# Attention softmax: shift writes negated scores and takes their minimum, and the weighting takes the sum's reciprocal and the gate itself

## The reference, cut to what matters

```
s = q . k - slope * distance
s = where(mask, s, NEG_INF)
m = max(s, axis=-1)
p = where(mask, exp(s - m), 0.0)
p = p / max(sum(p), 1e-30)
o = gate_c * o_c + gate_s * (p_s @ v_s) + gate_w * (p_w @ v_w)
```

## Time and profile before

| what | value |
|---|---|
| median of three runs | 1402.91 us (1398.88 to 1407.49) |
| the profiled execution | 1410.37 us |
| its span, first to last instruction | 1407.4 us |
| TensorE busy | 1309.8 us, 93% of the span |
| VectorE busy | 835.1 us, 59% |
| ScalarE busy | 408.9 us, 29% |
| GpSimd busy | 818.4 us, 58% |
| attention loop | about 889 to 1070 us of the span |
| line 1882, two instructions for each unit | 57.5 us busy, 128 instructions |
| line 1156 | 70.4 us busy, 128 instructions |
| mean granted clock of TensorE | 0.969 of 2.4 GHz |

### The profile page before, as it was taken

How to read it: one execution, slowest core, us unless ns; L and a number is a source line. 1 busy time by engine, 2 the same in 40 slices (tenths; PEclk the granted TensorE clock), 3 DMA queues, 4 the chain that set the end, 5 groups by cost and what they waited for, 6 DMA issues and landing times.

```text
span 1407.4 us, 22999 instructions
## 1 busy us (share of the span) xinstructions
PE 1309.8 (93%) x8136; PEld 1040.3 (74%) x8136; DVE 835.1 (59%) x1464; ACT 408.9 (29%) x782; POOL 818.4 (58%) x1041
## 2 busy tenths in 40 slices
PE   6999789899999999999989999898988998999986
PEld 4778688678887788888778797555556787878874
DVE  6977895569789311597418344577773649632223
ACT  4265100434301133212200121666673201231111
POOL 7677101587899877899776718100002875357862
PEclk9999898999999999999999999899999999999998
DMA  5222100143325433345492303000004459423321
GB/s 193 77 75 80 31 3 1 53 133 98 97 82 187 135 120 97 100 148 157 149 319 78 92 16 97 9 1 1 1 1 161 125 146 267 178 69 96 97 82 67
DMA packets 86480, 137.94 MB, mean 98 GB/s; under 512 B 16512, under 2 KB 34432, under 8 KB 85376
## 3 DMA queue, kind: packets, MB, share of 16 engines
q1 hardware_dynamic: 48384, 88.10, 20.7%
q10 hardware_dynamic: 38016, 48.71, 10.8%
HBM read 119.02 MB, written 20.91 MB: 99 GB/s over the span
## 4 chain that ended last, share of the span: by engine, by line
PE 74%; DVE 11%; issue 5%; POOL 3%; ACTq 3%; ACT 2%; DMA 2%; POOLq 0%; DVEq 0%
PE ps L373 18%; PE ps L374 18%; PE ps L375 18%; PE ps L718 3%; PE ps L730 3%; PE ps L707 2%; ACTq L1053 2%; POOL small L1286 1%; DVE acc L1360 1%; DVE bigB L1882 1%; PE ps L543 1%; PE ps L611 1%; PE ps L656 1%; PE ps L787 1%; PE ps L535 1%
## 5 line engine op out<-in xcount | busy, mean ns | idle before, releaser
L1289 POOL TENSOR_TENSOR wl<-raw,wh 128x512 fp32r<-128x512 f32 x336 | 497.6, 1481 | 26.9
L1286 POOL TENSOR_TENSOR small<-small 1x1 f32<-1x1 f32 x336 | 119.5, 356 | 340.4 <-PE ps L375 335.1
L373 PE MATMUL ps<-uH,wh 128*128 128x512 f32 x672 | 267.9, 399 | 17.6 <-DVE uL L1350 10.8
L375 PE MATMUL ps<-uH,wl 128*128 128x512 f32 x672 | 263.9, 393 | 0.0
L374 PE MATMUL ps<-uL,wh 128*128 128x512 f32 x672 | 263.9, 393 | 0.0
L1287 POOL CAST wh<-raw 128x512 fp32r<-128x512 f32 x336 | 203.3, 605 | 0.0
L373 PEld LDWEIGHTS ps<-uH,wh 128*128 128x128 f32 x672 | 127.6, 190 | 47.7 <-POOL wl L1289 9.9
L374 PEld LDWEIGHTS ps<-uL,wh 128*128 128x128 f32 x672 | 127.8, 190 | 27.4 <-issue 1.4
L375 PEld LDWEIGHTS ps<-uH,wl 128*128 128x128 f32 x672 | 127.6, 190 | 27.0
L373 PE MATMUL ps<-ffH,wh 128*128 128x512 f32 x256 | 101.3, 396 | 4.4 <-POOL wl L1289 4.3
L374 PE MATMUL ps<-ffL,wh 128*128 128x512 f32 x256 | 99.8, 390 | 0.0
(11 more groups left out here) (382 smaller groups left out, 2482.6 us busy)
## 6 DMA issues: line engine op xcount, KB each, us to landing
raw<-wstream SPq DMA_DIRECT2D x336, 256.0 KB, 2.6
b_powers_scratch<-bigB ACTq DMA_DIRECT2D x4, 1024.0 KB, 4.7
c_powers_scratch<-bigB ACTq DMA_DIRECT2D x8, 512.0 KB, 4.1
lags_scratch<-lag_rows_scratch ACTq DMA_DIRECT2D x8, 512.0 KB, 9.4
bigB<-b_powers_scratch ACTq DMA_DIRECT2D x4, 1024.0 KB, 8.2
bigB<-lags_scratch ACTq DMA_DIRECT2D x4, 1024.0 KB, 8.7
bigB<-c_powers_scratch ACTq DMA_DIRECT2D x4, 1024.0 KB, 11.3
hT<-x ACTq DMA_DIRECT2D x4, 512.0 KB, 7.4
```

The lines of the kernel that those rows point to most:

```text
L373: pe.matmul(out, lh, rh, start=first, stop=False)
L375: return pe.matmul(out, ll, rh, start=False, stop=last)
L1286: pool.tensor_tensor(small[0:1, 569 + j:570 + j], zero_ap[0:1], zero_ap[0:1], ALU.add)
L1289: pool.tensor_tensor(wl[:, j, :], raw[:, j, :], wh[:, j, :].bitcast(f32), ALU.subtract).then_inc(half_split, 1)
```

## The change

`shift` passes the factor -1.0 and the minimum where it passed 1.0 and the maximum, with the initial value +3e38. The instruction computes (scores + penalty) x factor and reduces that, so `prob` now holds the negated scores, and the reduced value is the negated maximum itself. It goes directly into `anmax`; line 1887, `amax` and the semaphore `at_m` are gone. ScalarE waits for `at_s` instead and computes exp(-1.0 x prob + anmax), which is the same number.

In `weigh` the multiplication of the reciprocal by the gate is gone. The scaling of the probabilities multiplies by two per-partition values, first the reciprocal, then the gate.

```diff
-                    act.wait_ge(at_m, n + 1)
+                    act.wait_ge(at_s, n + 1)
                     for half in range(2):
-                        i = act.activation(prob[:, n % 3, half, 0:W], prob[:, n % 3, half, 0:W], ACT.Exp,
+                        i = act.activation(prob[:, n % 3, half, 0:W], prob[:, n % 3, half, 0:W], ACT.Exp, scale=-1.0,
                                            bias=anmax[:, n % 3, half:half + 1], accum_out=asum[:, n % 3, half:half + 1])
...
                 for half in range(2):
                     i = dve.tensor_tensor_reduce(prob[:, u % 3, half, 0:W], ps[:, u % 2 * 2 + half, 0:W],
-                                                 dsl[t % 2][:, half, 512 - W:512], 1.0, -3e38, ALU.add, ALU.max,
-                                                 amax[:, u % 3, half:half + 1])
+                                                 dsl[t % 2][:, half, 512 - W:512], -1.0, 3e38, ALU.add, ALU.min,
+                                                 anmax[:, u % 3, half:half + 1])
                 i.then_inc(at_s, 1)
-                dve.wait_ge(at_s, u + 1)
-                dve.tensor_scalar(anmax[:, u % 3, :], amax[:, u % 3, :], -1.0, None, ALU.mult).then_inc(at_m, 1)
...
                 own(dve.reciprocal(asum[:, u % 3, :], asum[:, u % 3, :]))
-                own(dve.tensor_tensor(asum[:, u % 3, :], asum[:, u % 3, :], gate[:, qt, 1 + b, t::KT], ALU.mult))
                 for half in range(2):
-                    i = dve.tensor_scalar(prob[:, u % 3, half, 0:W], prob[:, u % 3, half, 0:W], asum[:, u % 3, half:half + 1], None, ALU.mult)
+                    i = dve.tensor_scalar(prob[:, u % 3, half, 0:W], prob[:, u % 3, half, 0:W], asum[:, u % 3, half:half + 1],
+                                          gate[:, qt, 1 + b, half * KT + t:half * KT + t + 1], ALU.mult, ALU.mult)
                 i.then_inc(at_p, 1)
```

More of the change, by code:

```diff
@@ L216, in build @@
         cm, cs_ = small[:, 500:516], small[:, 516:532]
-        amax = small[:, 532:538].rearrange("p (u b) -> p u b", b=2)
         anmax = small[:, 538:544].rearrange("p (u b) -> p u b", b=2)
@@ L268, in build @@
         ds_ready = sem("slopes_ready")
-        at_qk, at_s, at_m, at_e, at_p, at_t, at_ev, at_v, at_o = (sem(f"att_{n}") for n in
-            ("scores", "scores_read", "max", "exp", "probs", "transposed", "probsT", "value", "out"))
+        at_qk, at_s, at_e, at_p, at_t, at_ev, at_v, at_o = (sem(f"att_{n}") for n in
+            ("scores", "scores_read", "exp", "probs", "transposed", "probsT", "value", "out"))
         s_bc = sem("ssm_bc_loaded")
```

## The result

| | before | changed |
|---|---|---|
| median | 1402.75 us (1398.87 to 1407.49, 8 runs) | 1391.97 us (1388.92 to 1395.79, 8 runs) |
| profiled execution, its span | 1410.37, 1407.4 us | 1388.92, 1387.1 us |
| mean granted clock of it | 0.969 | 0.979 |

The ratio is 0.9923, 95% interval 0.9899 to 0.9946: 10.8 us less, where 8.6 were forecast. The difference is under 1%, but the interval leaves out 1. The time lies in the forecast's own bounds, 1390.7 to 1397.5.

What follows compares the result with a forecast made beforehand. TensorE, three quarters of the chain, bounded the kernel and waited 19.7 us for VectorE's scaled probabilities. Savings of 1.00 us for each t, 8.0 for eight, plus first and last unit made 8.6: 1402.9 to 1394 us, range 1386 to 1402.

Steps and rivals of the forecast that it cites:

- accumulator read to first scaling: In VectorE's weigh, the time between these two falls from 0.59 to 0.28 us, each unit's way 0.31 shorter.
- second pointer, both scalings of a unit: Each scaling in weigh reads a second per-partition value, costing 0 to 0.11 us a unit; 0.06 taken.
- turn(2): TensorE's wait for scaled probabilities at unit 2 (units 0 to 7) of each t: 0.51 us, coming 0.25 earlier.
- turn(4): TensorE's wait at unit 4: savings of weigh(2), (3) and (4) add up to 0.75 of 0.51 + 0.40 us.
- turn(6), GpSimd quiet: TensorE's wait at unit 6 without GpSimd interfering: 0.86 us before, coming another 0.25 earlier.
- turn(6) beside GpSimd: Six of the eight waits at unit 6, beside two GpSimd operations: 1.60 us each, saving 0.25 (0 to 0.6).
- first unit, last unit: At the two ends of the attention loop: the first unit saves about 0.33 us, the last 0.25.
- The ceiling: TensorE's 24 waits at line 718 for scaled probabilities, 19.7 us, the most a shorter VectorE can give directly.
- one of the signs: In VectorE's scaling: the prediction would be wrong if the 512-column scaling left 0.48 us.
- the clock rival: In the loop, shorter turn(6) waits remove two to four half-clock stretches, 5 to 10 us on top, 1388; chance 0.25.
- The slower rival: Two pointers push VectorE's scaling off its double rate: 4 to 6 us slower, 1408; chance 0.08.
- Nothing comes through: Behind each TensorE wait something else stands ready, ScalarE's copy or GpSimd, with added clock stretches: 1402 us; chance 0.12.

Runs made afterwards that it cites:

- e9: The changed kernel again, in 9 runs on one more chip: 1393.73 us against 1401.65 for the kernel before, ratio 0.9937, 7.9 us less.
- e10: The kernel before, unedited, executed once more for a second trace: 1397.19 us.
- experiments 1 and 2: The two halves of the change, each alone on the kernel before (e1 and e2): 1396.73 and 1398.03 us.
- e7: The kernel before with GpSimd's penalties two units later and four small dependent VectorE operations added in weigh(6): 1406.57 us, ratio 1.0024.
- e5: The changed kernel with a constant 0.5 in place of the gate's pointer in the scaling, leaving the gate out: 1388.44 us, ratio 0.9893.
- e1: The kernel before with the negated scores only, the gate still multiplied onto the reciprocal: 1396.73 us, ratio 0.9929.
- e2: The kernel before with only the gate multiply moved into the scaling, the negation kept: 1398.03 us, ratio 0.9942.
- e6: The changed kernel with GpSimd's penalties started two units later: 1387.85 us, ratio 0.9893 to the kernel before.

## Why the prediction was right, step by step

| step | forecast | measured |
|---|---|---|
| accumulator read to first scaling | 0.59 to 0.28 us | to 0.20 |
| second pointer, both scalings of a unit | 0.06 (0 to 0.11) | 0.12 |
| net for each unit | 0.25 | 0.27 |
| minimum for maximum | 0 | 0 (421 for 422 ns) |
| turn(2) | 0.25 | 0.27 |
| turn(4) | 0.50 (0.75 with turn(2)) | 0.40 (0.67); 0.26 in the first t |
| turn(6), GpSimd quiet | 0.25 | 0.27 |
| turn(6) beside GpSimd | 0.25 (0 to 0.6) | 0.23 |
| one t, no GpSimd | 1.00 | 0.94 |
| first unit, last unit | 0.33, 0.25 | 0.26, 0 |
| TensorE's waits in the loop | about 12 us | 12.9 (12.7 in e9) |
| VectorE busy | 21 less, minus the pointers' 7.7 | 13.6 less |
| sum | 8.6 | 7.4 in waits (20.3 in e10 to 12.9), 7.5 in full-clock time |

**The mechanism held.** At full clock the gain comes from the places named, each within 0.1 us of its share but for two: turn(4) of the first t, and the last unit, behind which TensorE does not wait for the scaling before or after the change. The row of before that was farthest from the operation, the 57 ns of a first pointer, was the price of the second one within 3 ns.

**Two errors hid each other.** The reciprocal was given 0.08 us behind the accumulator read and took 0.00, which made the unit's way 0.08 shorter than thought. For the pointer it took the middle between free and twice 57 ns, 0.06 a unit, and the upper end was the true one, 0.12. So the net was 0.39 less 0.12, where the forecast had 0.31 less 0.06: 0.27 for 0.25, right here partly by luck.

**The term that was mis-sized is turn(4).** Three savings of 0.25 were added up in front of it, 0.75, against 0.51 + 0.40 of waits. But turn(2) had taken its 0.27 already, and what turn(4) still waited was 0.40, not 0.50, and in the first t only 0.26. A saving beyond that only makes VectorE early. That is 0.9 of the 1.2 us by which the sum was high; the last unit, 0.25, is nearly all of the rest. In experiments 1 and 2 the cap shows as the 0.8 us at turn(4) by which the whole change saves less than its two halves added up.

**The ceiling and one of the signs.** The 19.7 us named as the ceiling were 20.3 without the swallowed wait. The 24 waits are three in each t, but in the first t they are not at turn(2), turn(4) and turn(6): there they are at turn(0), turn(4) and turn(6), and the swallowed one at turn(1), which gave the 0.27 that turn(2) did not. And one sign of being wrong came true without meaning it: the 512-column scaling left 0.48 and takes 0.54 with GpSimd quiet. The prediction's own price of 57 ns for a pointer would have put it there, so the sign contradicted the sum; it belonged at the 0.6 that the rival names.

**The surplus of the first comparison.** It gave 10.8 us and the second one 7.9. The shorter waits explain 7.4. In the second the clock's part is 1.3 us (33.2 for 34.5), not told from none. For the first the clocks of the kernel before are not on record except for the profiled execution, so that its 3 us more are clock is likely and not shown: the mean clock's share of the kernel before was 34.5, 36.1 and 39.7 us on three chips, and that of the changed kernel 32.5 and 33.2. How much of that the change itself brings, between nothing and some 3 us, stays open.

The trace on which the clock rival stood was an unlucky one: its half-clock stretches took 27.2 us of the loop, and in e10 the middle of the loop has none. In both traces of the changed kernel the four mid-loop stretches are gone too, as that rival's condition asked, and still the medians are 1392 and 1394, not 1388. One of the two traces of the kernel before had none to lose, and the first trace's clock's share, 43.6 us, lies above the mean of the kernel on every chip. The Trainium skill, TensorE: Matmul & The Clock Gate, section A second HAM failure mode: psum-queue depth-cycling, tells of a kernel whose short idles between groups of matmuls, often enough, swing the clock. The first trace of the kernel before agrees that this can happen; e7 and e10, with waits as long and 1.00 over 140 us each, show that it need not.

**The slower rival** would have shown in the slope from 128 to 256 columns: 0.52 ns a column with two pointers, as with one. The Trainium skill, Vector Engine (DVE) Microarchitecture Reference, section 5.1, names only conditions on the tensors for the engine's faster modes, and this trace agrees: a second pointer left the rate as it was. **"Nothing comes through"** is out by the 0.94 us for each t: no other wait took the place. ScalarE's copy never appears as what a turn waited for, and the six waits beside GpSimd gave their 0.23. That this is near the forecast's 0.25 is luck: each half of the change alone gave 0.22 there, so the savings of the parts did not add up to it.

## What to carry to other kernels

Price a shorter VectorE by the waits of the bottleneck that stand behind it, and cap each one at what it has left; two edits in front of the same wait need not add. Before two sums of waits are compared, look whether a half-clock stretch has swallowed one in either trace. Before an order is changed, ask what the instruction in the way was hiding: here one swap uncovered 72.7 us of waiting for ScalarE and cost 3.1%. When a wait is long at one place and short at its twins, look for another engine that starts on the same signal, and start it beside a unit that nobody waits for: one constant gave as much as half of the whole change. And a difference of a few us should be read in full-clock time beside the median before the clock is credited or blamed.

## What the runs showed of the hardware that was not expected

- An instruction that does not need the reduced value starts together with the accumulator read before it: both at 1035.20 us, where 0.08 was expected. The same reciprocal before the change stood 0.08 behind the start of the negation.
- A second per-partition pointer costs 60 ns an instruction (344 for 284 at 128 columns, 410 for 351 at 256), as the first did, and a constant in its place nothing (283 and 351 in e5).
- When a pair of 512-column scalings runs beside GpSimd's two operations, how long each engine is held varies much. With one pointer VectorE took 1.24 us and GpSimd 2.33 in e5, with two 1.78 and 1.52 in the changed kernel. But the number of pointers alone does not decide: in e1, with one, it was 1.58 and 1.53, and in e2, with two, 1.60 and 1.53. There the scaling starts 0.2 us behind GpSimd, in the other two with it. Why that makes a difference no run shows. The quiet pair takes 0.88 with one pointer and 1.00 with two, in e6:

```profile
948.14 1.00 DVE L1892 TENSOR_SCALAR bigB<-bigB,small 128x512 f32<-128x512 f32 x2
```

- The granted clock of one kernel differs from trace to trace at equal waits: 0.93 and 1.00 over the same 140 us of the kernel before.
